# Feed-forward entries: the norm's sum and power taken as whole rows

## Chip, cores and metric

The kernel runs on one core of a Trainium2 chip. The metric is the device time of one launch in microseconds (us), as the median of the runs. Engines are named as the profile names them: PE is TensorE (PEld its weight loads), DVE is VectorE, ACT is ScalarE, POOL is GpSimd, SP is SyncE.

## What is computed

The reference is a chain of two transformer blocks over 512 positions of width 1024, all in float32. The first block has two layers: layer 0 is a convolution module and a feed-forward network, layer 1 a differential attention and a feed-forward network; the second block has a sparse and a latent attention side by side, and a squared-ReLU network. What matters here is the entry of the two feed-forward networks of the first block, once per layer `l`:

```python
def rms_norm(x, g):
    x32 = x.astype(jnp.float32)
    y = x32 * lax.rsqrt(jnp.mean(x32 * x32, axis=-1, keepdims=True) + EPS)
    return (y * g.astype(jnp.float32)).astype(x.dtype)
...
        x = x + g_m * rms_norm(y, norm_g[l, 1])
        h = rms_norm(x, norm_g[l, 2]) * (1.0 + sc_f) + sh_f
        y = conv_ffn(h, ffn_w_in[l], ffn_dw[l], ffn_dwb[l], ffn_w_out[l])
```

## The kernel before

**Layout.** The residual stream `XT` lies transposed in SBUF: 8 tiles of 128 channels (partitions) by 512 positions (columns). A mean over channels is therefore a sum over partitions and over the 8 tiles, and its result is one number for each of the 512 positions.

**Products.** A large product takes float32 apart into a high and a low half (`whi`, `wlo` for weights, `Hh`, `Hl` for activations) and issues three matmuls for each 128x128 block (`mm3`, lines 289 to 291). ACT makes `whi` from the weights' staging buffer (line 316), DVE makes `wlo` (line 329), both at most two blocks ahead; SP fetches blocks into three staging buffers. All other PE work goes through `mm` (line 294), which takes its operands as they are. A plain float32 `mm` is shown by the profile as two passes, so that four `mm` appear as x8.

**Order of the work.** Every engine has its program written out by hand, stage by stage, with waits on semaphores by the name of a step. An engine takes its instructions in order, so one that waits holds back all behind it. Each stage gives the functions `tensor`, `scalar`, `vector`, `gpsimd` and `sync`.

**The entry of a feed-forward stage**, `f0` or `f1`, runs so:

1. DVE adds the last branch to `XT`, tile by tile (`add_to_x_dve`, lines 560 and 548), and ACT squares each tile into one of four buffers `sq` (line 425). A square waits until PE has used the tile that lay there four before.
2. PE sums the squares over the channels (`sums_alone`, with `one_sum`). For each tile it loads four 128x128 pieces of the squares as weights and moves one column of ones past each, which leaves a column per piece in PSUM bank 6: var by position in 128 rows and 4 columns. Filler matmuls that nobody reads (`fill`) stand between: 11 ahead, 2 after each tile, 5 after the last.
3. DVE turns the 128x4 sums into mean plus epsilon (`begin_norm`, line 499), POOL raises them to -0.5 (`power`, line 503).
4. PE spreads the 128x4 result over all partitions (`spread`: four matmuls of a broadcast column against the identity) into bank 7, as 128x512; then 9 fillers.
5. DVE multiplies each tile of `XT` by its gain and by bank 7 (`h_mul`, line 523), ACT adds the shift and rounds to `Hh` (`h_high`, line 535), DVE makes `Hl` (`h_low`, line 528). PE begins the first product as soon as tile 0 is there.

The same engines' queues hold nothing of another stage in this stretch: behind the norm stand, on DVE, `make_h_dve`, on PE the stage's products, on POOL the sums of squares of the stage's own exit (`gather_six`), hundreds of us later. `diag` and `part` are 128x512 buffers in SBUF; `part` collects squares on POOL at other norms, and `diag` is used much later, in the second block.

Of the kernel before, what the change touches and what calls it, by code (L numbers as in the profile page):

```python
# [12 lines left out]
ALU = mybir.AluOpType  # L13
# [3 lines left out]
P = 128  # L17
S = 512
D = 1024
DT = 8  # L20
# [4 lines left out]
EPS = 1e-6  # L25
# [189 lines left out]
def program(nc, ins, out):  # L215
# [3 lines left out]
    with ctx:  # L219
# [12 lines left out]
        pe, act, dve, pool, sp = Hand(), Hand(), Hand(), Hand(), Hand()  # L232

        gemm_done, norm_done, core_done = mark("pe_gemm"), mark("pe_norm"), mark("pe_core")
# [14 lines left out]
        NRM, SPREAD = 6, 7  # L249
# [43 lines left out]
        def mm(out_, l, r, start, stop):  # L293
            return pe.e.matmul(out_, l, r, start=start, stop=stop, skip_group_check=True)  # L294
# [67 lines left out]
        def open_bank(b, by):  # L362
            for m, step in left.get(b, ()):
                pe.wait_ge(*m[step])
            left[b] = by
# [84 lines left out]
        def one_sum(s, t):  # L450
            if t == 0:
                open_bank(NRM, [(dve_done, ("var", s))])
            pe.wait_ge(*act_done["sq", s, t])
            for tb in range(4):
                tok = mm(banks[NRM][:, tb:tb + 1], sq[t % 4][:, tb * P:(tb + 1) * P], ones[:, 0:1], t == 0 and tb == 0, t == DT - 1)
            tok.then_inc(*norm_done.up(("part", s, t), *([("sum", s)] if t == DT - 1 else [])))

        def sums_alone(s):
            fill(11)
            for t in range(DT):  # L460
                one_sum(s, t)
                fill(2 if t < DT - 1 else 5)

        def tile_sums(src, ready, start, stop):
            pe.wait_ge(*ready)
# [23 lines left out]
        def fill(n):  # L489
            j, b = pe.block, acc["ids"][acc["n"] % len(acc["ids"])]  # L490
            pe.wait_ge(*w_hi[j])
            for m, step in left.get(b, ()):
                pe.wait_ge(*m[step])
            for _ in range(n):
                mm(banks[b][:, :], whi[j % NW][:, 0:P], whi[j % NW][:, 0:S], True, True)

        def begin_norm(s, count, eps=EPS):
            dve.wait_ge(*norm_done["sum", s])
            dve.e.tensor_scalar(var4, banks[NRM][:, 0:4], 1.0 / count, eps, ALU.mult, ALU.add).then_inc(*dve_done.up(("var", s)))

        def power(s):
            pool.wait_ge(*dve_done["var", s])
            pool.e.tensor_tensor(rs4, var4, mhalf, ALU.pow).then_inc(*pool_done.up(("pow", s)))


        def spread(s, by, where=SPREAD, col=None, ready=None):
            if by:
                open_bank(where, by)
            col = rs4 if col is None else col
            pe.wait_ge(*(ready or pool_done["pow", s]))  # L510
            for tb in range(4):
                tok = mm(banks[where][:, tb * P:(tb + 1) * P], col[:, tb:tb + 1].to_broadcast([P, P]), ident[:, :], True, True)
            tok.then_inc(*norm_done.up(("spread", s)))
# [23 lines left out]
        def make_h_dve(ver, gain, shift, ready, r=None):  # L537
            for t in range(DT):
                h_mul(ver, t, gain[:, t:t + 1], ready + ([dve_done["h", ver, t - 4]] if t >= 4 else []), r)
                if t:  # L540
                    h_low(ver, t - 1, shift[:, t - 1:t])
            h_low(ver, DT - 1, shift[:, DT - 1:DT])
# [112 lines left out]
        def shift(l, ch):  # L655
            return modv[:, 48 * l + 8 * ch:48 * l + 8 * ch + 8]
# [668 lines left out]
        def ffn_stage(l, beside_dve, beside_act, beside_sp, before, after, then, inside=None):  # L1325
# [13 lines left out]

            def tensor():  # L1340
                sums_alone(s)
                spread(s, [(dve_done, ("hm", s, DT - 1))])
                fill(9)
                for part, (a, b) in enumerate(FFN_CHUNKS):
                    for j in range(a // 2, b // 2):
                        gemm(("up", l, j), f"ffn_in{l}", HX(s), 0, DT, 2, lambda m, j=j: [(dve_done, ("tap2", l, j, m))])
                    by = (act_done, "fo") if part == 0 else (dve_done, "fo")
                    down = [("down", l, part), f"ffn_out{l}", hidden(part), a, b]
                    if inside and part == 0:
                        tables = inside[0]()  # L1350
                    pe.within[:] = [tables] if inside else []
                    gemm(*down, 3, lambda m: [(by[0], (by[1], l, m))])
                    if part:
                        all_of(pe.within[0] if inside else ())
                        pe.within[:] = [sums_within(sy, 6)]
                    gemm(*down, 1, lambda m: [(by[0], (by[1], l, m))], 6)
                    pe.within[:] = []
                sum_last(sy)
                fill(4)
                spread(sy, [(dve_done, ("yr", after, DT - 1))])  # L1360
# [47 lines left out]

            def vector():
                scaled_gain(gain[l, 2], l, 4, 2)  # L1410
                begin_norm(s, D)
                make_h_dve(s, gain[l, 2], shift(l, 3), [dve_done["gain", l, 2], norm_done["spread", s]])
                work = beside_dve()
                dve.beside[:] = [work]
                for part, (a, b) in enumerate(FFN_CHUNKS):
                    for j in range(a // 2, b // 2):
                        def evac(m):
                            c = 2 * j + m % 2 + (22 if m > 1 else 0)
                            q, from_, o = 2 * j + m % 2 - a, bank((("up", l, j), m)), tmp[m]
                            dve.wait_ge(*act_done["tap0", l, j, m])  # L1420
                            dve.e.scalar_tensor_tensor(o[:, 1:S], from_[:, 0:S - 1], column(w3 + 44 + c), o[:, 1:S], ALU.mult,  # L1421
                                                       ALU.add).then_inc(*dve_done.up())
                            dve.wait_ge(*dve_done.now)
                            dve.e.scalar_tensor_tensor(o[:, 2:S], from_[:, 0:S - 2], column(w3 + c), o[:, 2:S], ALU.mult,
                                                       ALU.add).then_inc(*dve_done.up(("tap2", l, j, m)))
                            if m > 1:
                                dve.wait_ge(*act_done["silu", l, j, m - 2])
                                dve.wait_ge(*dve_done.now)
                                dve.e.tensor_tensor(o[:, :], o[:, :], tmp[m - 2][:, :], ALU.mult).then_inc(
                                    *dve_done.up(("gated", l, j, m - 2)))  # L1430
                                dve.wait_ge(*act_done["hid", l, part, q])
                                dve.e.tensor_tensor(HIDl[:, q, :], o[:, :], HIDh[:, q, :].bitcast(F32), ALU.subtract).then_inc(
                                    *dve_done.up(("lo", l, j, m - 2), ("hid", l, part, q)))

                        beside_gemm(dve, f"ffn_in{l}", 0, DT, 2, evac)

                    def evac_y(m):
                        if part == 1:
                            dve.wait_ge(*gemm_done[("down", l, 1), m])
                            dve.wait_ge(*act_done["fo", l, m])  # L1440
                            dve.e.tensor_tensor(Y[m], Y[m], bank((("down", l, 1), m))[:, :], ALU.add).then_inc(
                                *dve_done.up(("fo", l, m)))

                    if inside and part == 0:
                        tables = inside[2]()
                    dve.within[:] = [tables] if inside else []
                    beside_gemm(dve, f"ffn_out{l}", a, b, 3, evac_y)
                    if part:
                        all_of(dve.within[0] if inside else ())
                        dve.within[:] = []  # L1450
                    beside_gemm(dve, f"ffn_out{l}", a, b, 1, evac_y, 6)
                    dve.within[:] = []
                dve.beside[:] = []
                all_of(work)
                gated_gain(gain[l, 3], l, 5, 3)
                begin_norm(sy, D)
                add_to_x_dve(after, Y, gain[l, 3], [dve_done["gain", l, 3], norm_done["spread", sy]], then)

            def gpsimd():
                power(s)  # L1460
                pool.wait_ge(*norm_done["sum", s])
                gather_six(sy)
                power(sy)
                pool.wait_ge(*norm_done["sum", sy])
# [1198 lines left out]
```

## Time and profile before

| | |
|---|---|
| median of 3 runs | 2238.97 us (2238.93 to 2244.57) |
| profiled execution, its own time | 2241.62 us |
| span of the profiled execution | 2239.8 us |
| PE busy | 2142.1 us, 96% of the span |
| DVE, ACT, POOL busy | 1344.2, 871.1, 154.3 us |
| granted TensorE clock, mean | 0.969 of full speed |
| DMA | 225.03 MB, mean 100 GB/s |

A line of a timeline gives the start in us from the span's start, the duration, the engine, the line of the kernel, the operation, what it writes and reads, its shape, how many instructions were merged, and in brackets how long the engine stood idle before, with what ended that. Matmuls are pipelined, so the duration of one is longer than the distance between two. PEclk is the granted TensorE clock as a part of full speed: 1.00 is 2.4 GHz, 0.50 is 1.2 GHz.

### The profile page before, as it was taken

How to read it: one execution, taken by the hardware profiler on the slowest of the kernel's cores; microseconds unless marked ns; L12 is line 12 of the kernel's file. 1: busy time of each engine (PE TensorE's matmuls, PEld its weight loads, DVE VectorE, ACT ScalarE, POOL GpSimd, SP SyncE). 2: the span in 40 equal slices, each digit the busy share in tenths (PEclk: the TensorE clock that was granted, in tenths of full speed). 3: DMA queues.
4: the chain of work that ended last, by engine and by line, in shares of the span. 5: the costliest groups of instructions: out<-in, count | busy, mean ns of one | idle time of the engine just before them, and what ended most of it. 6: DMA issues, size and time to landing. Idle time of an engine off the chain costs nothing.

```text
span 2239.8 us, 26367 instructions
## 1 busy us (share of the span) xinstructions
PE 2142.1 (96%) x10663; PEld 1682.7 (75%) x10665; DVE 1344.2 (60%) x2279; ACT 871.1 (39%) x1453; POOL 154.3 (7%) x101
## 2 busy tenths in 40 slices
PE   5999999999999999899999999999889999999998
PEld 4755888888887876687887887777655578888886
DVE  7697468847844566647765566457865464633632
ACT  3355534423423255534432442323365443422421
POOL 0464100000010000020000001000000001000000
PEclk9999989999999999989999999999989999999999
DMA  8343225564531221012333323222113122333321
GB/s 297 123 150 100 76 66 188 188 213 164 183 99 57 76 67 38 29 48 81 94 103 110 94 90 125 64 75 77 45 46 117 29 76 77 112 94 94 94 94 66
DMA packets 67114, 225.03 MB, mean 100 GB/s; under 512 B 7217, under 2 KB 8113, under 8 KB 66993
## 3 DMA queue, kind: packets, MB, share of 16 engines
q1 hardware_dynamic: 64112, 218.11, 30.4%
q10 hardware_dynamic: 2880, 5.24, 0.6%
q8 instruction: 84, 1.38, 0.3%
q14 instruction: 38, 0.30, 0.0%
HBM read 215.98 MB, written 7.34 MB: 100 GB/s over the span
## 4 chain that ended last, share of the span: by engine, by line
PE 87%; DVE 7%; ACT 3%; issue 2%; DMA 0%; POOL 0%; SPq 0%; DVEq 0%; POOLq 0%; ACTq 0%
PE bank L289 24%; PE bank L291 23%; PE bank L290 23%; PE bank L294 16%; PE bank L794 2%; DVE wlo L329 1%; ACT whi L316 1%; DVE tmp L523 1%; DVE Hl L528 1%; ACT pr L767 1%; DVE sc L2053 0%; DVE steps L2051 0%; DVE pr L759 0%; DMA XT<-in_xT 0%; DVE part L1131 0%
## 5 line engine op out<-in xcount | busy, mean ns | idle before, releaser
L289 PE MATMUL bank<-Hh,whi 128*128 128x512 f32 x1632 | 653.0, 400 | 31.0 <-DVE wlo L329 7.4
L291 PE MATMUL bank<-Hh,wlo 128*128 128x512 f32 x1632 | 642.4, 394 | 0.0
L290 PE MATMUL bank<-Hl,whi 128*128 128x512 f32 x1632 | 641.7, 393 | 0.0
L329 DVE TENSOR_TENSOR wlo<-stg,whi 128x1024 fp32r<-128x1024 f32 (+1 forms) x299 | 358.7, 1204 | 413.6 <-ACT whi L316 413.0
L316 ACT ACTIVATE whi<-stg 128x1024 fp32r<-128x1024 f32 (+1 forms) x309 | 313.5, 1025 | 443.4 <-PE bank L291 438.3
L289 PEld LDWEIGHTS bank<-Hh,whi 128*128 128x128 f32 x1632 | 309.7, 190 | 107.3 <-issue 11.2
L291 PEld LDWEIGHTS bank<-Hh,wlo 128*128 128x128 f32 x1632 | 310.0, 190 | 66.6
L290 PEld LDWEIGHTS bank<-Hl,whi 128*128 128x128 f32 x1632 | 310.6, 190 | 62.1 <-issue 0.2
L289 PE MATMUL bank<-HIDh,whi 128*128 128x512 f32 x352 | 142.3, 404 | 0.0
L291 PE MATMUL bank<-HIDh,wlo 128*128 128x512 f32 x352 | 140.9, 400 | 0.0
L290 PE MATMUL bank<-HIDl,whi 128*128 128x512 f32 x352 | 139.3, 396 | 0.0
L1089 DVE SCALAR_TENSOR_TENSOR bank<-U,vec,bank 128x512 f32<-128x512 f32 x145 | 109.6, 756 | 5.1
L430 POOL TENSOR_TENSOR part<-sq 128x512 f32<-128x512 f32 x7 | 9.0, 1291 | 1366.4 <-ACT sq L425 1350.8
L291 PE MATMUL bank<-HID2h,wlo 128*128 128x512 f32 x256 | 102.1, 399 | 0.0
L290 PE MATMUL bank<-HID2l,whi 128*128 128x512 f32 x256 | 100.9, 394 | 0.0
L289 PE MATMUL bank<-HID2h,whi 128*128 128x512 f32 x256 | 100.5, 393 | 0.0
L1421 DVE SCALAR_TENSOR_TENSOR tmp<-bank,vec,tmp 128x511 f32<-128x511 f32 x88 | 65.9, 748 | 49.1 <-ACT tmp L1376 49.1
L607 DVE CUSTOM_DVE_ANT_0 raw<-raw,c_act 128x1024 f32<-128x1024 f32 x72 | 87.2, 1219 | 6.6 <-DMA raw<-in_mod_w 6.5
L1376 ACT ACTIVATE tmp<-bank,vec 128x512 f32<-128x512 f32 x88 | 67.7, 770 | 55.1 <-PE bank L291 55.1
L294 PE MATMUL bank<-U,dtap 128*128 128x512 f32 x186 | 83.7, 608 | 1.2 <-ACT dtap L1229 1.2
L291 PEld LDWEIGHTS bank<-HIDh,wlo 128*128 128x128 f32 x352 | 66.4, 189 | 15.7
L290 PEld LDWEIGHTS bank<-HIDl,whi 128*128 128x128 f32 x352 | 66.6, 189 | 15.3
(290 smaller groups left out, 2795.6 us busy)
## 6 DMA issues: line engine op xcount, KB each, us to landing
raw<-in_mod_w SPq DMA_DIRECT2D x96, 512.0 KB, 4.1
stg<-in_ffn_in SPq DMA_DIRECT2D x88, 512.0 KB, 4.1
stg<-in_ff SPq DMA_DIRECT2D x64, 512.0 KB, 3.6
stg<-in_ffn_out SPq DMA_DIRECT2D x40, 512.0 KB, 3.7
stg<-in_cm_w SPq DMA_DIRECT2D x24, 512.0 KB, 3.7
stg<-in_gates SPq DMA_DIRECT2D x16, 512.0 KB, 3.5
stg<-in_z_ch SPq DMA_DIRECT2D x12, 512.0 KB, 3.6
bias_kept<-out_b ACTq DMA_DIRECT2D x20, 256.0 KB, 2.1
```

Source lines behind the costliest of these rows:

```text
L289: pe.e.matmul(out_, l[0], r[0], start=start, stop=False, skip_group_check=True)
L290: pe.e.matmul(out_, l[0], r[1], start=False, stop=False, skip_group_check=True)
L291: return pe.e.matmul(out_, l[1], r[0], start=False, stop=stop, skip_group_check=True)
L294: return pe.e.matmul(out_, l, r, start=start, stop=stop, skip_group_check=True)
L316: act.e.activation(whi[j % NW][:, 0:n * c], stg[j % NSTG][:, 0:n * c], ACT.Copy).then_inc(*w_hi.up(j))
L329: hand.e.tensor_tensor(wlo[j % NW][:, 0:n * c], stg[j % NSTG][:, 0:n * c], whi[j % NW][:, 0:n * c].bitcast(F32), ALU.subtract).then_inc(*m ...
L523: dve.e.scalar_tensor_tensor(tmp[t % 4][:, :], x_tile(t), gain, r[:, :], ALU.mult, ALU.mult).then_inc(*dve_done.up(("hm", ver, t)))
L607: dve.e.tensor_tensor_reduce(raw[j % NRAW][:, :], raw[j % NRAW][:, :], c_act[:, :], 1.0, 0.0, ALU.mult, ALU.add, modv[:, a:a + 1]).then_in ...
L794: tok = pe.e.transpose(banks[b][:, kb * P:(kb + 1) * P], p[:, kb * P:(kb + 1) * P], ident[:, :])
L1089: dve.e.scalar_tensor_tensor(a[:, :] if k < CONV - 1 else C[:, t, :], U[:, t, k:k + S], vcol("cm_dw", 8 * k + t), a[:, :], ALU.mult, ALU.a ...
L1376: act.e.activation(at_, bank((("up", l, j), m))[:, :], ACT.Identity, bias=column(bcol + c), scale=column(w3 + 88 + c)).then_inc(*act_done. ...
L1421: dve.e.scalar_tensor_tensor(o[:, 1:S], from_[:, 0:S - 1], column(w3 + 44 + c), o[:, 1:S], ALU.mult, ALU.add).then_inc(*dve_done.up())
```

## The change

At the entries of the two feed-forward stages the operands of the sum change places: a 128x128 matrix of ones is the weight, and the squares, 512 columns, move past it. Each output row then holds the sums of all 512 positions, the same in every partition. DVE makes mean plus epsilon of the 128x512 rows (`begin_row`), into `part`; POOL raises the whole 128x512 to -0.5 into `diag` (`power_row`), with the exponent as a broadcast column; DVE's `h_mul` reads `diag` where it read bank 7. The spread is gone, and the fillers are 11 ahead, 1 after each tile, 3 after the last, and 16 after those. POOL's instruction `power` of these two norms is gone too. Nothing else changes: the exits of the same stages and all other norms keep the narrow power and the spread.

```diff
         def sums_alone(s):
+            open_bank(NRM, [(dve_done, ("row", s))])
             fill(11)
             for t in range(DT):
-                one_sum(s, t)
-                fill(2 if t < DT - 1 else 5)
+                pe.wait_ge(*act_done["sq", s, t])
+                mm(banks[NRM][:, :], ones[:, :], sq[t % 4][:, :], t == 0, t == DT - 1).then_inc(
+                    *norm_done.up(("part", s, t), *([("sum", s)] if t == DT - 1 else [])))
+                fill(1 if t < DT - 1 else 3)
...
+        def begin_row(s, count):
+            dve.wait_ge(*norm_done["sum", s])
+            dve.e.tensor_scalar(part[:, :], banks[NRM][:, :], 1.0 / count, EPS, ALU.mult, ALU.add).then_inc(*dve_done.up(("row", s)))
+
+        def power_row(s):
+            pool.wait_ge(*dve_done["row", s])
+            pool.e.tensor_tensor(diag[:, :], part[:, :], mhalf[:, 0:1].to_broadcast([P, S]), ALU.pow).then_inc(*pool_done.up(("pow", s)))
...
             def tensor():
                 sums_alone(s)
-                spread(s, [(dve_done, ("hm", s, DT - 1))])
-                fill(9)
+                fill(16)
...
             def vector():
                 scaled_gain(gain[l, 2], l, 4, 2)
-                begin_norm(s, D)
-                make_h_dve(s, gain[l, 2], shift(l, 3), [dve_done["gain", l, 2], norm_done["spread", s]])
+                begin_row(s, D)
+                make_h_dve(s, gain[l, 2], shift(l, 3), [dve_done["gain", l, 2], pool_done["pow", s]], diag)
...
             def gpsimd():
-                power(s)
-                pool.wait_ge(*norm_done["sum", s])
+                power_row(s)
                 gather_six(sy)
                 power(sy)
```

## Rows read from the trace of the kernel before

**Rows 1.** The page, parts 1 and 4: engines' busy time, chain that ended last
```profile
PE 2142.1 (96%) x10663; PEld 1682.7 (75%) x10665; DVE 1344.2 (60%) x2279; ACT 871.1 (39%) x1453; POOL 154.3 (7%) x101
...
PE 87%; DVE 7%; ACT 3%; issue 2%; DMA 0%; POOL 0%; SPq 0%; DVEq 0%; POOLq 0%; ACTq 0%
```

**Rows 2.** Windows of the two entries: us, busy by engine, PEclk, DMA share, GB/s
```profile
280.00:312.00 32.00, 31.23 (x134) 27.28 (x135) 15.40 (x27) 7.82 (x12) 2.02 (x2) 0.69 0.00 1
984.00:1020.00 36.00, 35.53 (x179) 30.50 (x177) 21.10 (x36) 10.99 (x17) 2.02 (x2) 0.81 0.04 14
```

**Rows 3.** Timeline, first entry: start us, us, engine, line, operation, tiles, count, idle before
```profile
293.10 1.23 ACT L425 ACTIVATE sq<-XT 128x512 f32<-128x512 f32 x2 [0.63 <-DVE XT L548]
...
301.14 1.70 PE L294 MATMUL bank<-ones,sq 128*128 128x1 f32 x8
...
302.88 0.16 DVE L499 TENSOR_SCALAR small<-bank 128x4 f32<-128x4 f32 x1 [9.14 <-PE bank L294]
303.12 1.01 POOL L503 TENSOR_TENSOR small<-small 128x4 f32<-128x4 f32 x1 [21.90 <-DVE small L499]
...
307.00 1.41 DVE L523 SCALAR_TENSOR_TENSOR tmp<-XT,gains,bank 128x512 f32<-128x512 f32 x2 [3.96 <-PE bank L294]
...
309.44 0.47 PE L289 MATMUL bank<-Hh,whi 128*128 128x512 f32 x1 [0.40 <-DVE Hl L528]
```

**Rows 4.** Timeline, second entry, same columns
```profile
995.68 0.95 PE L294 MATMUL bank<-ones,sq 128*128 128x1 f32 x8
...
997.04 0.95 PE L294 MATMUL bank<-ones,sq 128*128 128x1 f32 x8
...
1000.59 1.23 ACT L425 ACTIVATE sq<-XT 128x512 f32<-128x512 f32 x2 [0.63 <-DVE XT L548]
...
1005.98 0.16 DVE L499 TENSOR_SCALAR small<-bank 128x4 f32<-128x4 f32 x1 [4.75 <-PE bank L294]
1006.29 1.01 POOL L503 TENSOR_TENSOR small<-small 128x4 f32<-128x4 f32 x1 [17.74 <-DVE small L499]
...
1010.10 1.40 DVE L523 SCALAR_TENSOR_TENSOR tmp<-XT,gains,bank 128x512 f32<-128x512 f32 x2 [3.96 <-PE bank L294]
```

**Rows 5.** Timeline of the convolution on PE: 14 passes over 512 columns
```profile
104.02 6.18 PE L294 MATMUL bank<-U,dtap 128*128 128x512 f32 x14
```

**Rows 6.** Groups by line and shape, DVE: count, busy us, mean ns, idle before
```profile
L523 DVE SCALAR_TENSOR_TENSOR tmp<-XT,gains,RBk 128x512 f32<-128x512 f32 x8 | 5.9, 746 | 0.0
...
L1085 DVE TENSOR_SCALAR bank<-U,vec 128x512 f32<-128x512 f32 x5 | 4.1, 812 | 0.1
```

**Rows 7.** Groups by line and shape, POOL, same columns
```profile
L615 POOL TENSOR_TENSOR raw<-raw,c_act 128x1024 f32<-128x1024 f32 x24 | 56.4, 2364 | 7.0 <-DMA raw<-in_mod_w 6.6
L434 POOL TENSOR_TENSOR part<-part,sq 128x512 f32<-128x512 f32 x28 | 38.4, 1370 | 126.5 <-ACT sq L425 123.7 <-ACT sq L1221 1.8
L503 POOL TENSOR_TENSOR small<-small 128x4 f32<-128x4 f32 x21 | 23.9, 1140 | 485.1 <-DVE small L499 485.1
...
L430 POOL TENSOR_TENSOR part<-sq 128x512 f32<-128x512 f32 x7 | 9.0, 1291 | 1366.4 <-ACT sq L425 1350.8 <-ACT sq L1221 15.6
```

**Rows 8.** Line 503 alone: shortest, median and longest duration in ns
```profile
L503 POOL TENSOR_TENSOR small<-small x21: 1006/1007/1929, 18.6 to 2229.6; 128x4 f32<-128x4 f32 x21
```

**Rows 9.** Timeline, start of the kernel: PE restarts after idling
```profile
31.13 0.77 PE L289 MATMUL bank<-Hh,whi 128*128 128x512 f32 x1 [6.12 <-DVE C L1123]
...
31.70 0.63 PE L290 MATMUL bank<-Hl,whi 128*128 128x512 f32 x1
...
32.12 0.63 PE L291 MATMUL bank<-Hh,wlo 128*128 128x512 f32 x1
...
37.52 0.39 PE L289 MATMUL bank<-Hh,whi 128*128 128x512 f32 x1
...
37.74 0.40 PE L290 MATMUL bank<-Hl,whi 128*128 128x512 f32 x1
```

**Rows 10.** Window of the same restart, columns as in rows 2
```profile
32.00:36.00 4.00, 4.00 (x11) 3.03 (x11) 3.96 (x12) 0.81 (x1) 0.00 (x0) 0.50 0.57 204
```

## The prediction

> **What bounds the kernel now.** I read the page first: PE is busy 96% of the span and carries 87% of the chain of work that ended last; POOL is busy 7% [rows 1]. So a shift of the start of a large product moves the end by as much, and a POOL instruction costs nothing unless PE waits for it. Next the windows of the two entries: both hold little else than the norm, at a mean granted clock of 0.69 and 0.81 and with next to no DMA [rows 2]. Then the timelines, where the reader is to follow one chain: last square, last sum, power, spread, first multiply, first product. At the first entry the squares end at 293.10 + 1.23 = 294.33, but the sum is ready only at 302.88, because PE is behind: its clock has fallen, and the passes of one tile take 1.70 us where they take 0.95 at full clock [rows 3, 4]. The first multiply starts at 307.00, the first product at 309.44. At the second entry the squares end at 1001.82, the sum is read at 1005.98, the first multiply starts at 1010.10 [rows 4]. These chains are on the path: nobody has other work in them.
>
> **The sum.** Removed: 8 passes with one column each for a tile. Added: one float32 matmul of 512 columns. The convolution has just this shape: 14 passes take 6.18 us, so (6.18 - 0.61) / 13 = 0.43 us a pass with 0.61 for the last to land [rows 5]. A tile is two passes, 0.86 us, with one filler about 1.1, against 1.36 before [rows 4]; squares come every 1.26, so PE keeps up at full clock. The sum is ready 0.1 + 0.43 + 0.61 = 1.1 us after the last square: 295.4 and 1002.9. Saved: 7.4 and 3.0 us. If the clock still fell to half, a tile would take 2.2 us and most of this would be lost; the range keeps that end.
>
> **DVE's row.** 0.16 us [rows 3] becomes a 128x512 tensor_scalar; the nearest is line 1085 at 0.81 us, which writes PSUM [rows 6]. I take 0.7, between that and other DVE instructions of this size: plus 0.5 at each entry.
>
> **The spread.** From the end of the power to the first multiply it took 307.00 - 304.13 = 2.9 us [rows 3] and 2.8 [rows 4]; a semaphore of about 0.1 is left. Saved: 2.8 and 2.7. The multiply reads SBUF in place of PSUM; line 523 with such an operand, in another stage, takes 746 ns [rows 6], and two of it at this entry 1.41 us [rows 3], so nothing. The 16 fillers run while POOL works and hide there (16 x 0.23 = 3.7 us); they cost only if the power is shorter than about 1.5 us. POOL's later queue (the exit's sums) is hundreds of us away, and DVE's queue behind the row is only what needs the power.
>
> So without the power's own growth: first entry 7.4 - 0.5 + 2.8 = 9.7, second 3.0 - 0.5 + 2.7 = 5.2, together **14.9 us gained**.
>
> **The power.** This is the one price the trace does not show, and it decides. Line 503 raises 128x4 in 1006 ns at its shortest and 1007 in the median [rows 8]. POOL's ordinary two-input instructions cost 1291 ns at 128x512 and 2364 at 128x1024 [rows 7]: (2364 - 1291) / 512 = 2.1 ns a column and 0.22 us fixed. At four columns an ordinary one would take 0.23 us; the power takes 0.78 more. Three readings:
> - Lower end: the 0.78 is all set-up, and columns then stream as in an addition: 1.29 + 0.78 = 2.1 us; at the very least 1.29.
> - Upper end: everything grows with the columns: 1.007 / 4 x 512 = 129 us.
> - Per column: (1007 - 218) / 4 = 197 ns, so 0.22 + 512 x 0.197 = **101 us**.
> I take 101. A power is a long chain of multiplications and additions in software; that such a chain runs at the pace of one addition is implausible, and the one width measured is best read as four times its price. Nothing in the rows shows whether columns overlap, so all between stays in the range.
>
> The Trainium skill (GPSIMD Engine Reference, Performance pitfalls for Q7 kernels) says that a chain of dependent float32 operations pays 4 cycles for each unless independent ones are interleaved; no row here shows it, and it leans to the costly side.
>
> **PE's clock after the wait.** PE runs out of fillers some 4 us into a wait of 100, and is idle. At the start of the kernel PE idles 6.12 us; afterwards its matmuls stand 0.42 apart until about 37.2, then 0.22 [rows 9], at a clock of 0.50 [rows 10]. That is 6.1 us at half pace, of which 6.1 x (1 - 0.23 / 0.43) = 2.8 lost. I add 2.8 at each entry; it is an estimate, the idle here being much longer.
>
> **Sum.** 2 x (101 - 1.0) = +200.0; -14.9; +5.6: **+190.7 us** on the profiled span of 2239.8, about 8.5%. The profiled execution's own time, 2241.62, is 2.7 over the median, within the spread of the runs, so I add the same to the median: 2239 + 191 = **2430 us**. With X for the power in us, the time is 2239 + 2X - 16.9 + 5.6, without the 5.6 below about X = 5.
>
> **Rivals.**
> - *The power streams* (ends faster). X between 1.3 and 8.4 us: at 2.1 us, 2239 - 16.9 + 4.2 = 2226; at 1.29, 2225. It decides below X = 8.45, or 5.7 if the clock falls too. For it: 1.0 us at four columns may be one price per instruction; POOL's other instructions do have one; and no wider power stands in the trace to contradict. Against it: the excess of 0.78 us over an ordinary instruction would pay for 0.78 / 0.0021 = 370 columns of an addition. Beside it, the Trainium skill (GPSIMD Engine Reference, Elementwise: side-by-side cycle accounting) gives about 2.6 cycles at 1.2 GHz per column for two-input work on this engine; the trace's 2.1 ns a column agrees, for additions and products. If it held for a power, this rival would be the outcome. Chance 0.18, all but 0.02 of it clear of no change.
> - *The power overlaps columns in part*, as where the four columns are a short remainder of a wider loop: the 0.78 us would buy, say, 16 columns, so X = 0.22 + 32 x 0.78 = 25 us and the time 2239 + 50 - 11.3 = 2278. X from 8.4 to 60, 2239 to 2348. For it: four columns are too few to fill any pipeline. Chance 0.30.
> - *The price is per column*, my forecast: X 60 to 129, 2348 to 2486. Chance 0.52.
> - *It does not do what it says*: the half clock stays during the sums, as today. That gives back at most the 10 us of the sum term and leaves all signs but the first rival's edge. It changes no chance by more than 0.02.
>
> **Range and chances.** Low end: X = 11.5, 2239 + 23 - 11 = 2251, rounded down to 2248; it leaves out the faster rival and the first slice of the second. High end: the upper bound, 2239 + 258 - 11 = 2486, rounded to 2490. The forecast case's own range is 2348 to 2490. A change of less than 0.3% (6.7 us) can hardly be told from none here; that needs X between 5 and 9. Faster 0.16, same 0.03, slower 0.81.
>
> **What would show it.** In the profile after, the POOL group diag<-part 128x512, two instructions, gives X at once: about 101,000 ns if I am right, 2,000 or 25,000 if a rival is. Line 499's count falls by two and no ident,small matmuls stand in the entries. PE's idle before line 289 grows by about X at each entry, released by POOL or by DVE's Hl behind it; the slices of the span around 350 and 1150 show PE near 0 and a clock of 0.5. The sum should be ready 1.1 us after the last square. I am wrong if X is under 60 us; and if X is small and the time does not fall by about 14 us, the sum or spread term was wrong.

## The result, and the profile after

The changed kernel takes 2388.45 us in the median of 4 runs (2385.45 to 2393.22), the kernel before 2240.79 (2238.93 to 2244.57). The ratio is 1.0654, with a 95% interval of 1.063 to 1.0678: slower by some 148 us. The profiled execution took 2393.22 us, with a span of 2391.4, 151.6 above the span before.

The page of the changed kernel, its first lines, two of the rows of 40 slices, and the shares of the chain that ended last:

```profile
span 2391.4 us, 26129 instructions
...
PE 2135.3 (89%) x10547; PEld 1666.6 (70%) x10549; DVE 1345.6 (56%) x2279; ACT 871.4 (36%) x1453; POOL 316.3 (13%) x101
...
PE   6999906999999999890599999999989999999998
...
PEclk9998957999999999895799999999989999999999
...
PE 81%; POOL 7%; DVE 6%; ACT 3%; issue 2%; DMA 0%; SPq 0%; DVEq 0%; POOLq 0%; ACTq 0%
```

Against [rows 1] PE's busy time fell by 7 us while the span rose by 152: nothing became more expensive on PE; it waits. Two holes in PE's row, at the sixth and seventh and at the nineteenth and twentieth slice, are the two entries, and POOL, which was nowhere in the chain, now holds 7% of it: 0.07 x 2391 = 167 us. The group of POOL's instructions by line and shape (count, busy us, mean ns, idle before) says which:

```profile
L511 POOL TENSOR_TENSOR diag<-part,small 128x512 f32<-128x512 f32 x2 | 163.9, 81928 | 30.0 <-DVE part L507 30.0
```

**81.93 us for one power of 128x512.** In the timeline of the first entry (start us, us, engine, line, what it does, idle before) everything that [rows 3] showed between the last square and the power has become short, and then comes the wait:

```profile
290.55 1.23 ACT L425 ACTIVATE sq<-XT 128x512 f32<-128x512 f32 x2 [0.63 <-DVE XT L560]
...
293.48 0.69 DVE L507 TENSOR_SCALAR part<-bank 128x512 f32<-128x512 f32 x1 [2.29 <-PE bank L294]
294.26 81.93 POOL L511 TENSOR_TENSOR diag<-part,small 128x512 f32<-128x512 f32 x1 [14.63 <-DVE part L507]
```

```profile
376.29 1.42 DVE L535 SCALAR_TENSOR_TENSOR tmp<-XT,gains,diag 128x512 f32<-128x512 f32 x2 [82.11 <-POOL diag L511]
...
378.73 0.76 PE L289 MATMUL bank<-Hh,whi 128*128 128x512 f32 x1 [80.93 <-DVE Hl L540]
...
379.29 0.63 PE L290 MATMUL bank<-Hl,whi 128*128 128x512 f32 x1
...
379.71 0.63 PE L291 MATMUL bank<-Hh,wlo 128*128 128x512 f32 x1
...
383.11 0.39 PE L290 MATMUL bank<-Hl,whi 128*128 128x512 f32 x1
...
383.34 0.40 PE L291 MATMUL bank<-Hh,wlo 128*128 128x512 f32 x1
```

The squares end at 290.55 + 1.23 = 291.78, DVE's row starts at 293.48, the power at 294.26; it ends at 376.19 and the first multiply starts at 376.29. From last square to first multiply it is 84.5 us, where it was 12.7. The second entry, to be read against [rows 4]:

```profile
1072.60 1.23 ACT L425 ACTIVATE sq<-XT 128x512 f32<-128x512 f32 x2 [0.63 <-DVE XT L560]
...
1075.54 0.69 DVE L507 TENSOR_SCALAR part<-bank 128x512 f32<-128x512 f32 x1 [2.29 <-PE bank L294]
1076.38 81.93 POOL L511 TENSOR_TENSOR diag<-part,small 128x512 f32<-128x512 f32 x1 [15.41 <-DVE part L507]
```

```profile
1158.41 1.42 DVE L535 SCALAR_TENSOR_TENSOR tmp<-XT,gains,diag 128x512 f32<-128x512 f32 x2 [82.17 <-POOL diag L511]
...
1160.85 0.76 PE L289 MATMUL bank<-Hh,whi 128*128 128x512 f32 x1 [81.00 <-DVE Hl L540]
```

From 1073.83 to 1158.41 it is 84.6, where it was 8.3. The two differences, 71.8 and 76.3 us, make 148.1 of the span's 151.6. The rest, 3.5 us, is about what PE's clock costs behind the two waits (2.0 and 1.8 us, worked out below); the other stretches moved by -2.6 to +1.5 us and nearly cancel. In the first product above the matmuls from 379.29 on stand 0.42 to 0.43 apart, those from 383.11 on 0.23. The windows (us, busy by engine, PEclk, DMA share, GB/s) show the granted clock at full during the new sums and at 0.73 on average in the 13 us that follow the wait:

```profile
283.00:294.00 11.00, 10.71 (x29) 4.55 (x28) 8.71 (x15) 5.00 (x8) 0.00 (x0) 1.00 0.01 1
376.00:389.00 13.00, 10.27 (x36) 8.33 (x37) 12.25 (x18) 7.64 (x10) 0.18 (x1) 0.73 0.00 0
```

### The profile page after: what moved, and what is told of

Same layout as the page of the kernel before. It is cut to its first block, busy times and chain, and to the rows that moved or that the text cites. A ratio compares the mean times of both kernels' runs of the same rounds, so it can differ in the third digit from the quotient of the medians.

```text
span 2391.4 us, 26129 instructions
## 1 busy us (share of the span) xinstructions
PE 2135.3 (89%) x10547; PEld 1666.6 (70%) x10549; DVE 1345.6 (56%) x2279; ACT 871.4 (36%) x1453; POOL 316.3 (13%) x101
## 4 chain that ended last, share of the span: by engine, by line
PE 81%; POOL 7%; DVE 6%; ACT 3%; issue 2%; DMA 0%; SPq 0%; DVEq 0%; POOLq 0%; ACTq 0%
PE bank L289 22%; PE bank L291 22%; PE bank L290 22%; PE bank L294 14%; POOL diag L511 7%; PE bank L806 2%; DVE wlo L329 1%; ACT whi L316 1%; ACT pr L779 1%; DVE tmp L535 0%; DVE Hl L540 0%; DVE sc L2063 0%; DVE steps L2061 0%; DVE pr L771 0%; DMA XT<-in_xT 0%
## 5 line engine op out<-in xcount | busy, mean ns | idle before, releaser
L511 POOL TENSOR_TENSOR diag<-part,small 128x512 f32<-128x512 f32 x2 | 163.9, 81928 | 30.0 <-DVE part L507 30.0
L535 DVE SCALAR_TENSOR_TENSOR tmp<-XT,gains,diag 128x512 f32<-128x512 f32 x16 | 11.8, 745 | 164.3 <-POOL diag L511 164.3
L547 ACT ACTIVATE Hh<-tmp,modv 128x512 fp32r<-128x512 f32 x24 | 17.2, 726 | 184.0 <-DVE tmp L535 184.0
```

What stands on the lines that cost most here:

```text
L511: pool.e.tensor_tensor(diag[:, :], part[:, :], mhalf[:, 0:1].to_broadcast([P, S]), ALU.pow).then_inc(*pool_done.up(("pow", s)))
```

## The experiments

**1. How the power's price grows.** The wide power is cut into seven widths, behind one ordinary product.

```diff
-            pool.e.tensor_tensor(diag[:, :], part[:, :], mhalf[:, 0:1].to_broadcast([P, S]), ALU.pow)...
+            pool.e.tensor_tensor(diag[:, 0:4], part[:, 0:4], mhalf, ALU.mult).then_inc(*pool_done.up())
+            pool.wait_ge(*pool_done.now)
+            for a, b in ((0, 4), (4, 12), (12, 28), (28, 60), (60, 128), (128, 256), (256, 512)):
+                tok = pool.e.tensor_tensor(diag[:, a:b], part[:, a:b], mhalf[:, 0:1].to_broadcast([P, b - a]), ALU.pow)
+            tok.then_inc(*pool_done.up(("pow", s)))
```

> The wide power is cut into seven instructions of 4, 8, 16, 32, 68, 128 and 256 columns, and one ordinary product of 4 columns is put before them. My theory, a price per column: a line through 1.007 us at 4 columns and 81.93 at 512 gives 0.37 us fixed and 0.159 us a column, so 1.0, 1.6, 2.9, 5.5, 11.2, 20.8 and 41.2 us, in all 84 us, and the time 2 to 4 us above the changed kernel. Rival, a loop with a wide body and a slow remainder: 16 and 32 columns cost clearly less for each column than 4 and 8, or the durations go in steps. Rival, the 0.78 us of the narrow power over an ordinary instruction is a set-up: then 8 columns cost about as much as 4. The product of 4 columns should take about 0.23 us.

2391.28 us (one run). The groups of the first entry by shape; the number just before the second bar is the duration of one in ns:

```profile
L514 POOL TENSOR_TENSOR diag<-part,small 128x256 f32<-128x256 f32 x1 | 41.1, 41115 | 0.0
L514 POOL TENSOR_TENSOR diag<-part,small 128x128 f32<-128x128 f32 x1 | 20.7, 20717 | 0.0
L514 POOL TENSOR_TENSOR diag<-part,small 128x68 f32<-128x68 f32 x1 | 11.2, 11217 | 0.0
L514 POOL TENSOR_TENSOR diag<-part,small 128x32 f32<-128x32 f32 x1 | 5.4, 5414 | 0.0
L514 POOL TENSOR_TENSOR diag<-part,small 128x16 f32<-128x16 f32 x1 | 2.9, 2894 | 0.0
L514 POOL TENSOR_TENSOR diag<-part,small 128x8 f32<-128x8 f32 x1 | 1.6, 1633 | 0.0
...
L514 POOL TENSOR_TENSOR diag<-part,small 128x4 f32<-128x4 f32 x1 | 1.0, 1006 | 0.1
L511 POOL TENSOR_TENSOR diag<-part,small 128x4 f32<-128x4 f32 x1 | 0.2, 206 | 15.5 <-DVE part L507 15.5
```

From 4 to 8 columns the step is 0.157 us a column, from 8 to 16 and from 16 to 32 it is 0.158, from 128 to 256 it is 0.159. The price is a straight line with about 0.37 us at no columns. 16 columns lie on the same line as 4 and 8, so there is no wide body with a slow remainder, and 8 cost 0.63 us more than 4, so the narrow power was not mainly set-up. An ordinary product of 4 columns takes 0.21 us; the power's own start costs only 0.16 more. All durations came as expected, within 0.1 us, and so did the time.

**2. Everything but the power.** POOL multiplies in its place, so the norm's scale is left out.

```diff
-            pool.e.tensor_tensor(diag[:, :], part[:, :], mhalf[:, 0:1].to_broadcast([P, S]), ALU.pow)...
+            pool.e.tensor_tensor(diag[:, :], part[:, :], mhalf[:, 0:1].to_broadcast([P, S]), ALU.mult)...
```

> POOL's wide power becomes a wide product with the same operands; the power is left out, so the norm's scale is not taken. My theory: the power's duration alone is the loss, and the rest of the change gains 14.9 us less 0.3 for the product's growth: POOL 1.3 us at each entry, the time about 14 us below the kernel before, 2226 against 2240.8, ratio 0.9936. Rival, the rest of the change gains nothing (sum and spread were hidden or the clock falls elsewhere): 2238 to 2243.

2224.67 us in the median of 4 against 2241.86 for the kernel before, ratio 0.9924 (0.9903 to 0.9945). Its timeline at the first entry:

```profile
292.07 1.23 ACT L425 ACTIVATE sq<-XT 128x512 f32<-128x512 f32 x2 [0.63 <-DVE XT L560]
...
295.01 0.69 DVE L507 TENSOR_SCALAR part<-bank 128x512 f32<-128x512 f32 x1 [2.29 <-PE bank L294]
295.78 1.04 POOL L511 TENSOR_TENSOR diag<-part,small 128x512 f32<-128x512 f32 x1 [15.41 <-DVE part L507]
296.92 1.41 DVE L535 SCALAR_TENSOR_TENSOR tmp<-XT,gains,diag 128x512 f32<-128x512 f32 x2 [1.22 <-POOL diag L511]
```

Same line, same operands, same width, 1.04 us in place of 81.93: the loss lies in the operation, not in moving rows of this width. From last square (293.30) to first multiply it is 3.6 us, at the second entry 3.7 (991.46 to 995.14), so 9.1 and 4.6 us are gained, 13.7 together; the span is 13.9 below the span before. The rest of the change does what was forecast, and the rival, that it gains nothing, is out.

**3. Are the exponents to blame?** The power reads a full operand in place of one column again and again.

```diff
...
+            pool.e.memset(diag[:, :], -0.5).then_inc(*pool_done.up())
+            pool.wait_ge(*pool_done.now)
             pool.wait_ge(*dve_done["row", s])
-            pool.e.tensor_tensor(diag[:, :], part[:, :], mhalf[:, 0:1].to_broadcast([P, S]), ALU.pow)...
+            pool.e.tensor_tensor(diag[:, :], part[:, :], diag[:, :], ALU.pow)...
```

> The exponents no longer come from one column read again for every position: POOL fills the buffer with -0.5 before the sum is ready, and the power reads it as an ordinary 128x512 operand and writes over it. My theory, the price is the power's own arithmetic for each column: 81.9 us at each entry as in the changed kernel, give or take 0.3 (the product with the broadcast column took 1.04 us, an addition of two full operands 1.29), and 2388 to 2393 us. Rival, the repeated reading of one column costs: clearly under 80 us.

2385.17 us (one run), 3 us under the expected times and just under the fastest run of the changed kernel (2385.45). The group reads:

```profile
L515 POOL TENSOR_TENSOR diag<-part,diag 128x512 f32<-128x512 f32 x2 | 164.3, 82173 | 30.3 <-DVE part L507 30.3
```

82.17 us is 0.24 more than with the repeated column; ordinary instructions show a like step, 1.04 us for the product with a repeated column [experiment 2] and 1.29 for an addition of two full operands [rows 7]. The repeated column was no cost.

**4. The sum alone.** The new sum with the narrow power: DVE takes the diagonal pieces out of the whole rows.

```diff
-            dve.e.tensor_scalar(part[:, :], banks[NRM][:, :], 1.0 / count, EPS, ALU.mult, ALU.add)...
+            for tb in range(4):
+                dve.e.tensor_tensor_reduce(diag[:, tb * P:(tb + 1) * P], banks[NRM][:, tb * P:(tb + 1) * P], ident[:, :], 1.0, 0.0, ALU.mult,
+                                           ALU.add, var4[:, tb:tb + 1]).then_inc(*dve_done.up())
+            dve.wait_ge(*dve_done.now)
+            dve.e.tensor_scalar(var4, var4, 1.0 / count, EPS, ALU.mult, ALU.add)...
...
-            pool.e.tensor_tensor(diag[:, :], part[:, :], mhalf[:, 0:1].to_broadcast([P, S]), ALU.pow)...
+            pool.e.tensor_tensor(rs4, var4, mhalf, ALU.pow)...
...
-                fill(16)
+                fill(7)
+                spread(s, [(dve_done, ("hm", s, DT - 1))])
+                fill(9)
```

> The new sum alone: whole rows from PE, then DVE multiplies each 128x128 piece by the identity and adds it up, which gives the 128x4 that POOL raises in the narrow form, and PE spreads as before. My theory: the sum's gain stays (7.4 and 3.0 us), the four DVE pieces cost 1.3 us at each entry, and the spread runs at full clock and is some 0.5 us shorter: 8 to 9 us gained, 2232, ratio 0.996. Rival, the sum's gain came from the dropped fillers or is lost in the chain of DVE pieces: ratio 0.999 to 1.001.

2224.19 us against 2241.86, ratio 0.9932 (0.9913 to 0.9951), 8 us lower than expected. First entry:

```profile
291.37 1.23 ACT L425 ACTIVATE sq<-XT 128x512 f32<-128x512 f32 x2 [0.63 <-DVE XT L564]
...
294.31 0.29 DVE L508 CUSTOM_DVE_ANT_0 diag<-bank,ident 128x128 f32<-128x128 f32 x1 [2.29 <-PE bank L294]
...
295.27 0.17 DVE L511 TENSOR_SCALAR small<-small 128x4 f32<-128x4 f32 x1
295.52 1.01 POOL L515 TENSOR_TENSOR small<-small 128x4 f32<-128x4 f32 x1 [15.99 <-DVE small L511]
...
296.68 1.13 PE L294 MATMUL bank<-ident,small 128*128 128x128 f32 x8
...
297.84 1.41 DVE L539 SCALAR_TENSOR_TENSOR tmp<-XT,gains,bank 128x512 f32<-128x512 f32 x2 [2.40 <-PE bank L294]
```

The chain is 5.2 us from last square (292.60) to first multiply, and 5.3 at the second entry (989.93 to 995.23): 7.4 and 3.0 gained, 10.4 in all, somewhat more than expected. The DVE pieces take 0.96 from the first to the narrow tensor_scalar, and the spread, now at full clock, brings the first multiply 1.3 us behind the power's end, where it took 2.9 [rows 3]. The time fell by more than that: 0.68% is 15 us, and the span is 17.5 lower. Stretches that no edit touches differ by some us between profiled executions: from the POOL power of the norm that opens the attention (at 720.27 us in the kernel before) to that of the first attention head (846.11) it is 125.8 us before, 122.3 here and between 122.2 and 125.6 in the other kernels. That is 3.5 of the 7.1 us by which the span fell further than the entries explain, and it goes with PE's clock: the stretch takes 124.2 to 125.8 us in the six traces where the granted clock in it is 0.96, the kernel before among them, and 122.2 to 122.7 in the five where it is 0.99. Two executions of one kernel, that of experiment 7, fell on either side, at 124.2 and 122.7 us. What sets the clock there is not shown. The interval's near end, 11 us, comes close to what the entries show.

**5. The root on ACT.** One instruction from PSUM in place of DVE's row, POOL's power and the spread; `epsc` is a column of epsilon that POOL fills at the start.

```diff
             def scalar():
+                act.wait_ge(*pool_done["epsc"])
+                act.wait_ge(*norm_done["sum", s])
+                act.e.activation(diag[:, :], banks[NRM][:, :], ACT.Abs_reciprocal_sqrt, bias=epsc, scale=1.0 / D).then_inc(*act_done.up(("pow", s)))
...
-                fill(16)
+                fill(9)
...
-                begin_row(s, D)
-                make_h_dve(s, gain[l, 2], shift(l, 3), [dve_done["gain", l, 2], pool_done["pow", s]], diag)
+                make_h_dve(s, gain[l, 2], shift(l, 3), [dve_done["gain", l, 2], act_done["pow", s]], diag)
```

> The new sum, and ACT takes the reciprocal root of the whole rows straight from PSUM, in one instruction, with 1/1024 as scale and epsilon as bias; DVE's row, POOL's power and the spread are gone. My theory: 0.8 us for the instruction and a load of its table of perhaps 1.3 us ahead of it, in place of DVE's 0.7 and POOL's 82: 12 to 16 us below the kernel before, 2225 to 2229, ratio 0.993 to 0.995. Rival, the tables have to be loaded again behind it, for the square before it and the Silu after it, and eat the gain: ratio over 0.997.

2221.55 us against 2241.86, ratio 0.9913 (0.9889 to 0.9937), some 4 us better than expected. First entry:

```profile
290.84 1.23 ACT L426 ACTIVATE sq<-XT 128x512 f32<-128x512 f32 x2 [0.63 <-DVE XT L561]
...
292.09 1.28 ACT L1378 ACT_TABLE_LOAD   x1
...
293.77 0.69 ACT L1378 ACTIVATE diag<-bank,small 128x512 f32<-128x512 f32 x1 [0.40 <-PE bank L295]
294.56 1.42 DVE L536 SCALAR_TENSOR_TENSOR tmp<-XT,gains,diag 128x512 f32<-128x512 f32 x2 [3.08 <-ACT diag L1378]
```

The root takes 0.69 us, and its table is loaded in 1.28 us as soon as ACT has its last square behind it (292.07), so it ends at 293.37, 0.4 us before the sum is there: the whole load hides beside PE's last passes. The first multiply starts 2.5 us after the last square at both entries. Behind it the Silu's table has to be loaded again in each network (two loads at that line where the kernel before has one, 1.28 us each), 14 us after the root, beside the products; the chain pays nothing visible for it: from the first multiply to the power at the first network's exit it is 370.7 us in both kernels. The rival of tables that eat the gain is out.

**6. PE kept awake through the wait.**

```diff
-                fill(16)
+                fill(365)
```

> The changed kernel with 365 fillers in place of 16 behind the sum, so that PE is busy until about the first multiply of h, some 83 us. My theory: the first products start at full clock, where the changed kernel shows 4.3 and 3.8 us of half clock behind its idle time; that saves 2.1 and 1.8 us, and the power's 81.9 us stay. By the trace the first ten matmuls of each product stand 0.23 us apart in place of 0.43. Rival, the clock has nothing to do with the idle time: they stay 0.43 apart. If the fillers run longer than I count, the product starts late by the difference.

2382.70 us (one run), 5.8 below the median of the changed kernel, where 3.9 was forecast; the stretch named in experiment 4 is 2.5 us shorter in this trace than in that of the changed kernel. Windows of the first entry, in the wait and behind it:

```profile
294.00:376.00 82.00, 80.92 (x357) 66.66 (x356) 1.54 (x3) 0.89 (x2) 80.23 (x1) 1.00 0.00 0
376.00:389.00 13.00, 11.74 (x48) 8.87 (x49) 12.67 (x18) 7.49 (x10) 0.00 (x0) 1.00 0.08 18
```

The clock is full in the wait and stays full in the 13 us behind it, where the changed kernel had 0.73, and the first matmuls stand 0.23 apart. At the second entry it came otherwise:

```profile
1150.00:1153.00 3.00, 1.08 (x6) 0.61 (x5) 2.87 (x5) 1.40 (x3) 0.00 (x0) 1.00 0.01 3
1153.00:1156.00 3.00, 3.00 (x10) 2.40 (x9) 3.00 (x5) 1.80 (x3) 0.00 (x0) 0.62 0.03 5
1156.00:1159.00 3.00, 3.00 (x12) 2.37 (x12) 3.00 (x6) 1.80 (x3) 0.00 (x0) 0.81 0.00 0
```

PE's idle time before the first product was 1.9 us at both entries. Here the clock was still full in the first five matmuls and then fell, under matmuls 0.23 apart: 0.62 and 0.81 on average in the next 6 us, about 3.4 us at half. So the idle time is the cause at the first entry, and something that these windows don't tell apart takes the clock at the second. My expectation held for one entry of two.

**7. Without fillers, new sum.** Experiment 5 without the filler after each of the first seven tiles.

```diff
-                fill(1 if t < DT - 1 else 3)
+                if t == DT - 1:
+                    fill(3)
```

> The version in which ACT takes the root, without the filler after each of the first seven tiles. My theory: passes over 512 columns keep the clock at full by themselves, although PE now idles some 0.4 us of every 1.26: granted clock 0.95 or more between the first square and the first product, and a time within 4 us of the version with fillers. Rival, the fillers kept the clock: it falls to 0.5 in that stretch at one entry at least, as in the kernel before, and the sum is ready 3 us or more later.

2218.86 us (one run), and the window from the first square to the first product:

```profile
283.00:297.00 14.00, 12.36 (x32) 5.17 (x31) 11.02 (x19) 8.37 (x12) 0.00 (x0) 1.00 0.01 1
```

The clock is full with PE busy 12.4 of 14 us and only 32 matmuls: with the fillers between the tiles gone it did not fall. At the second entry a window from 979 to 988 us shows 1.00 too, with PE busy 8.2 of 9 us. The same holds in every trace with the new sum, with fillers or without: nine traces, and from the first square to the last the granted clock is 1.00 at both entries. The same kernel with five runs:

> The root on ACT with no fillers between the first seven tiles, the same kernel as e8_bare, now timed in five rounds for an interval. My theory: 20 to 24 us below the kernel before, ratio 0.989 to 0.991, no worse than with the fillers (0.9913). Rival, the single time of 2218.86 was a lucky one: ratio 0.993 or more.

2218.12 us in the median of 5 against 2243.45, ratio **0.9887** (0.9872 to 0.9902), 25 us below the kernel before and slightly more than forecast. This version beats both kernels. Over experiment 5 it shows no gain that is clear of the intervals.

```profile
292.18 1.23 ACT L426 ACTIVATE sq<-XT 128x512 f32<-128x512 f32 x2 [0.63 <-DVE XT L562]
...
293.43 1.28 ACT L1379 ACT_TABLE_LOAD   x1
...
294.88 0.69 ACT L1379 ACTIVATE diag<-bank,small 128x512 f32<-128x512 f32 x1 [0.17 <-PE bank L295]
```

ACT reads the sum 294.88 - 293.41 = 1.5 us after the last square, 0.2 sooner than with the fillers, since PE does not have to finish one before its last tile.

**8. Without fillers, old sum.** The kernel before, with the same fillers taken out.

```diff
-                fill(2 if t < DT - 1 else 5)
+                if t == DT - 1:
+                    fill(5)
```

> The kernel before with its own sum (squares as weights, one column of ones moved) and no fillers between its first seven tiles: what dropping fillers alone would give. My theory: the clock still falls to 0.5 in the sum, because passes of one column do not hold it; a tile then takes 2.04 us in place of 2.56 at half clock, so the sum is ready up to 3 us earlier at the first entry and under 1 us at the second: ratio 0.998 to 1.000. Rival, the fillers were the brake and the exchange of operands gives nothing of its own: the sum is ready within 2 us of the last square at both entries, ratio 0.995 or less.

2233.68 us in the median of 6 against 2243.45, ratio 0.996 (0.9947 to 0.9973), between the two expectations. Windows and timeline of the first entry; the single window that follows them is of the kernel before:

```profile
287.00:290.00 3.00, 2.58 (x20) 2.41 (x19) 3.00 (x6) 1.40 (x3) 0.00 (x0) 0.85 0.03 5
290.00:293.00 3.00, 3.00 (x16) 3.00 (x15) 3.00 (x6) 1.74 (x4) 0.00 (x0) 0.50 0.00 0
```

```profile
289.28 8.69 PE L294 MATMUL bank<-ones,sq 128*128 128x1 f32 x40 [0.21 <-ACT sq L425]
...
292.38 1.23 ACT L425 ACTIVATE sq<-XT 128x512 f32<-128x512 f32 x2 [0.63 <-DVE XT L549]
...
298.01 0.16 DVE L500 TENSOR_SCALAR small<-bank 128x4 f32<-128x4 f32 x1 [4.99 <-PE bank L294]
```

```profile
290.00:293.00 3.00, 3.00 (x12) 2.75 (x12) 3.00 (x6) 1.26 (x2) 0.00 (x0) 0.50 0.00 0
```

The clock falls to half during the passes of one column, and PE is busy 3.00 of 3.00 us behind the fall, in this kernel and in the kernel before; five tiles then take 8.69 us. Ahead of the fall PE was busy 2.58 of 3 us here. Over the squares the granted clock is 0.74 and 0.76 at the two entries here and 0.75 and 1.00 in the kernel before, which at its second entry kept the clock over the same one-column passes and lost it 1.5 us after the last square. The sum is read 298.01 - 293.61 = 4.4 us after the last square, where it was 8.5 with the fillers: 4 us were the fillers' own, and I had said up to 3. At the second entry it is 4.3, as before (4.2). So at the first entry more than half of what the new sum gains (8.5 to 1.7 us) was to be had by dropping fillers, and the rest and all of the second entry's (4.2 to 1.7) is the exchange of operands. The measured 9.8 us is more than the 4 that the entries show. In the traces, whose spans differ by 11.0, another 3.7 lie in the stretch named in experiment 4, at a clock of 0.99 for 0.96; the rest I can't place.

## Why the prediction was right, and by how much it missed

The direction, the mechanism and the place were right: the power's price per column decides, PE waits for it at both entries, and the rest gains what it was said to. The forecast was 2430 us, the median is 2388, inside the case's own range of 2348 to 2490. That the price is per column was a judgement, with a chance of 0.52 on it; no row of the kernel before decided it.

- **The power** is the term that was mis-sized: 101 us forecast, 81.93 measured. I took an ordinary instruction's fixed 0.22 us [rows 7] off the narrow power and divided the rest by four: 197 ns a column. Experiment 1 shows the power's own fixed part to be 0.37 us and the column 0.159. With only four columns in the sample, 0.15 us of unseen fixed cost became 38 ns a column and 19 us an instruction. Twice 19 is 38 us, and 2430 - 38 = 2392: that is nearly all of the miss. That a power is a long chain of arithmetic in software, the reason given for the choice, is not shown by any run; the runs show only the price of a column, 0.159 us.
- **The other readings.** The line through the one width, with no set-up of its own, was the right reading. Both rivals fell by experiment 1: no streaming (8 columns cost 1.63 us, not 1.0) and no overlap of columns (16 cost 2.89, not 1.0). The Trainium skill (GPSIMD Engine Reference, Elementwise: side-by-side cycle accounting) gives about 2.6 cycles a column for two-input work. The traces agree for two full operands, 2.1 ns or by the page's 1.2 GHz 2.5 cycles a column [rows 7]; a product with a repeated column costs less, (1.04 - 0.21) / 508 = 1.6 ns or 2.0 cycles, and a power is far off, 1.2 x 159 = 191 cycles. These cycles are estimates from the page's clock.
- **The sum.** Forecast ready 1.1 us after the last square, measured 1.7 at both entries (291.78 to 293.48, 1073.83 to 1075.54): the last two squares come only 0.6 us apart, and PE still has a tile and a filler before the last. Saved 6.9 and 2.5, for 7.4 and 3.0 forecast. The fear that the clock falls all the same did not come true: 1.00 in the window. The sizes of this term and of the clock's were both a little off, and small beside the power's.
- **DVE's row** took 0.69 us, for 0.7. **The spread**'s place is taken by 0.10 us between POOL and DVE, as forecast.
- **The sum of these** was 14.9 us forecast with the power left out of account; experiment 2 gives 13.9 on the span, at 1.04 us of POOL, which by the forecast's formula is 2 x 1.04 - 16.9 = -14.8.
- **The clock after the wait.** Forecast 6.1 us at half pace and 2.8 lost at each entry, from the kernel's start [rows 9, 10]. Measured 4.3 us at the first entry and 3.8 at the second, so 2.0 and 1.8 lost. The mechanism holds at the first entry by experiment 6; at the second that experiment is undecided.

With the measured power and nothing else changed the forecast's formula gives 2239 + 163.9 - 11.3 = 2391.6.

Two edges of the forecast are loose: its formula with the clock's 5.6 in it gives 2245 us at X = 8.4, not 2239, and its low end of 2251 became 2248, which is no rounding. Neither touches the outcome.

## What to carry to other kernels

An instruction seen at one small width has two unknowns, a fixed part and a price per column; divide by the width only after asking what kind of work it does, and where the answer decides, measure two widths first. Here POOL's power was work per column, and four columns cost 1.006 us whether the 128 partitions held 128 different values [rows 8] or one value 128 times (experiment 1). So a result that has been broadcast is the worst form in which to give it one: take the root on the narrow form, or on ACT, which took 0.69 us for the whole rows where its square takes 0.63. And where a sum runs behind its inputs, look at the clock it runs at: in this kernel the one-column passes kept PE busy and still lost the clock at both entries, and at the first the fillers only made the sum later.

## What I had not expected of the hardware

- ACT's reciprocal root of 128x512 from PSUM takes 0.69 us, and its table 1.28 us, all of it hidden behind the wait for the sum; in experiment 7 the root starts 1.5 us after the last square ends, with the load in between. The Silu's reload runs beside the products.
- The granted clock was 0.50 during passes of one column with PE busy 3.00 of 3.00 us, with fillers and without, and 1.00 during passes of 512 columns with PE busy 12.4 of 14 us.
- At the second entry of experiment 6 the clock fell for about 3.4 us under dense matmuls, a few us after 84 us at full clock.
- The same untouched stretch differs between executions by up to 3.6 us (122.2 to 125.8), with a granted clock of 0.99 or 0.96 in it, which is more than some of the terms weighed here.
